# Squares of four chunks added on GpSimd ahead of TensorE's column sums, and the last block's last weights in two token halves

## The reference

```
def rmsnorm(x, g):
    xf = x.astype(jnp.float32)
    y = xf * lax.rsqrt(jnp.mean(xf * xf, axis=-1, keepdims=True) + EPS)
    return (y * g.astype(jnp.float32)).astype(x.dtype)
...
for l in range(DEPTH):
    mod = (jax.nn.silu(cond) @ ada_w[l] + ada_b[l])[:, None, :]
    sh_m, sc_m, g_m, sh_f, sc_f, g_f = jnp.split(mod, N_MOD, axis=-1)
    h = rmsnorm(x, norm_mix_g[l]) * (1.0 + sc_m) + sh_m
    ...
    x = x + g_m * y
    h = rmsnorm(x, norm_ffn_g[l]) * (1.0 + sc_f) + sh_f
    x = x + g_f * (jnp.square(jax.nn.relu(h @ ffn_w1[l])) @ ffn_w2[l])
return rmsnorm(x, final_norm_g), outs_f, outs_b
```

## Time and profile before

| | |
|---|---|
| median of the runs shown (lowest) | 1217.7 us (1216.96) |
| the profiled execution | 1218.6 us |
| its span on the slowest core (core 2) | 1217.3 us; the others 1211.5 to 1215.9 |
| PE / DVE / ACT / POOL busy | 1110.2 / 461.1 / 423.4 / 112.8 us |
| mean granted TensorE clock | 0.981 of 2.4 GHz on core 2, 0.983 to 0.985 on the others |

### The profile page before, as it was taken

The page is one execution under the profiler, slowest core; times in us unless marked ns, Lnnn a source line. Parts: engine busy times, 40 slices in busy tenths (PEclk is TensorE's granted clock), DMA queues, the critical chain, the costliest instruction groups (busy, mean ns, idle before and its releaser), DMA issues.

```text
span 1217.3 us, 16072 instructions; the slowest of 8 cores (1211.5 to 1217.3 us)
## 1 busy us (share of the span) xinstructions
PE 1110.2 (91%) x6516; PEld 552.7 (45%) x6516; DVE 461.1 (38%) x817; ACT 423.4 (35%) x789; POOL 112.8 (9%) x150
## 2 busy tenths in 40 slices
PE   0368998887999999999999999999999999999996
PEld 0133576665444444444444444443444444444442
DVE  0333477676464222222222444825532222222235
ACT  1355576664465320013310551124643100332022
POOL 0122355442000000000000000000000000000000
PEclk9988999998999999999999999999999999999998
DMA  9870844338116844854674344141403431340004
GB/s 163 159 186 1 146 88 123 68 72 212 66 37 103 137 72 69 138 97 69 113 125 70 49 69 69 35 75 30 68 3 69 69 48 22 70 70 1 1 32 176
DMA packets 13446, 99.46 MB, mean 82 GB/s; under 512 B 1499, under 2 KB 5083, under 8 KB 7356
## 3 DMA queue, kind: packets, MB, share of 16 engines
q0 software_dynamic: 6272, 78.91, 37.8%
q1 hardware_dynamic: 7100, 19.52, 4.8%
HBM read 165.27 MB, written 7.86 MB: 142 GB/s over the span
## 4 chain that ended last, share of the span: by engine, by line
PE 87%; DVE 3%; DMA 3%; ACT 3%; POOL 2%; issue 1%; SPq 0%; POOLq 0%; ACTq 0%; DVEq 0%
PE psf L322 87%; DMA sb_X<-xT 3%; POOL sb_B L915 1%; ACT sb_hT L336 1%; DVE sb_ntm L342 1%; ACT sb_A L336 1%; DVE sb_B L342 1%; DVE sb_X L342 1%; POOL sb_X L915 0%; DVE sb_A L339 0%; ACT L336 0%; DVE sb_X L339 0%; ACT sb_B L336 0%; PE psf L910 0%; ACT sb_lnr L336 0%
## 5 line engine op out<-in xcount | busy, mean ns | idle before, releaser
L322 PE MATMUL psf<-sb_hT,sb_slot 128*128 128x512 bf16 (+1 forms) x2472 | 557.3, 384 | 32.6 <-ACT sb_hT L336 22.6
L322 PEld LDWEIGHTS psf<-sb_hT,sb_slot 128*128 128x128 bf16 (+1 forms) x2472 | 241.3, 99 | 326.6 <-issue 14.0
L322 PE MATMUL psf<-sb_A,sb_slot 128*128 128x512 bf16 x1632 | 362.3, 380 | 0.0
L322 PEld LDWEIGHTS psf<-sb_A,sb_slot 128*128 128x128 bf16 x1632 | 159.6, 98 | 192.5 <-issue 1.1
L336 ACT ACTIVATE sb_relu<-psf 128x512 bf16<-128x512 f32 x192 | 113.6, 595 | 356.2 <-PE psf L322 356.2
L342 DVE SCALAR_TENSOR_TENSOR sb_X<-psf,sb_modT,sb_X 128x512 f32<-128x512 f32 x144 | 108.1, 750 | 277.7 <-PE psf L322 277.6
L339 DVE TENSOR_TENSOR sb_A<-sb_relu 128x512 bf16<-128x512 bf16 x192 | 81.7, 425 | 240.3 <-ACT sb_relu L336 239.9
L336 ACT ACTIVATE sb_B<-sb_X 128x512 bf16<-128x512 f32 x96 | 57.2, 624 | 193.2 <-DVE sb_X L342 156.6
L322 PE MATMUL psf<-sb_slot,sb_hT 128*128 128x192 bf16 (+2 forms) x672 | 92.2, 292 | 6.3 <-DVE sb_B L342 6.3
L336 ACT ACTIVATE sb_hT<-sb_ntm,sb_modT 128x512 bf16<-128x512 f32 x96 | 67.9, 721 | 38.5 <-DVE sb_ntm L342 37.7
L342 DVE SCALAR_TENSOR_TENSOR sb_ntm<-sb_X,sb_gscT,sb_rstd 128x512 f32<-128x512 f32 x96 | 70.3, 749 | 25.3 <-ACT sb_rstd L336 21.1
(11 more groups left out here) (115 smaller groups left out, 619.7 us busy)
## 6 DMA issues: line engine op xcount, KB each, us to landing
sb_slot<-w POOLq DMA_DIRECT2D x16, 2048.0 KB, 16.0
sb_slot<-adaw POOLq DMA_DIRECT2D x12, 2048.0 KB, 15.3
sb_X<-xT SPq DMA_DIRECT2D x6, 1024.0 KB, 8.5
yT<-sb_X SPq DMA_DIRECT2D x12, 512.0 KB, 2.7
sb_X<-xT POOLq DMA_DIRECT2D x4, 1024.0 KB, 20.2
sb_X<-xT SPq DMA_DIRECT2D x4, 512.0 KB, 28.9
sb_slot<-evH POOLq DMA_DIRECT2D x1, 2048.0 KB, 14.2
sb_slot<-dft SPq DMA_DIRECT2D x1, 2048.0 KB, 15.0
```

Of the source, the lines that this page charges most:

```text
L322: T.op("pe", lambda: nc.tensor.matmul(out, l, r, start=start, stop=stop), reads=R, writes=W, sig=stop if sig is None else sig)
```

## The change

The squares stay on ACT, one for each chunk. In the four later norms POOL then adds the squares of two neighbouring chunks in f32 and two such pairs into one bf16 tile, so that TensorE has one statistic matmul for four chunks (`stat4`). Its lag is 5 groups in `outproj` and 3 in the MLPs' last half, and `norm_end` is put off as far. The first norm keeps `stat`.

In the last `w2` piece of the second MLP the third block (`m = 1`) is done in two halves of 256 tokens (`final_halves`): four groups of 16 matmuls of 256 columns for the first half, then four for the second. The added squares of its channels 0 to 3 are held back (`hold=True`) and go in by one matmul of 256 columns for each half; channels 4 to 7 have a statistic matmul of 256 columns for each chunk and half, with lag 1. `fin` is the final norm of a half: `Ln`, `Exp`, eight DVE operations of 256 columns, and four transfers, of which the second half gives two to ACT's queue.

```
+        def padd(o, a, b):
+            T.op("pool", lambda: nc.gpsimd.tensor_tensor(out=o[0], in0=a[0], in1=b[0], op=ALU.add),
+                 reads=[a[1], b[1]], writes=[o[1]])
+
+        def stat4(m, c, lag, hold=False):
...
+            s_ = qnext("s", 0)
+            act(s_[0], xT[m][:, c, :], AF.Square, [xT_b[m][c]], [s_[1]])
+            st = qr["m"][m]
+            st.append(s_)
+            if c % 2 == 1:
+                a, b = st.pop(), st.pop()
+                o = qnext("p", 1)
+                padd(o, b, a)
+                st.append(o)
+            if c % 4 == 3:
+                a, b = st.pop(), st.pop()
+                o = qnext("q", 2)
+                padd(o, b, a)
+                if hold:
+                    qr["hold"] = o
+                    return
+                pe_defer(lag, lambda: mm(ps[:], onesb[:], o[0], [o[1], on_b], [pb], start=(c == 3), stop=(c == 7), sig=True))
...
-                stat(m, oc, 2)
+                stat4(m, oc, 5)
                 if oc == 7:
                     pend.append(m)
-                    pe_defer(2, lambda: norm_end(m, nxt))
+                    pe_defer(5, lambda: norm_end(m, nxt))
...
+        def final_halves(m, w, slb, aT, aT_b, l):
...
+            def fin(hs, q, sp_, spb):
+                act(lnr[:, hs], sp_[:, hs], AF.Ln, [spb, on_b], [lnr_b], bias=cst[:, 0:1])
+                act(rstd[:, hs], lnr[:, hs], AF.Exp, [lnr_b], [rstd_b], scale=-0.5)
+                for c in range(8):
+                    stt(xT[m][:, c, hs], xT[m][:, c, hs], pp[:, PP_GFIN + c:PP_GFIN + c + 1], rstd[:, hs], ALU.mult, ALU.mult,
+                        [xT_b[m][c], rstd_b, pp_b], [xT_b[m][c]])
+                    if c % 2 == 1:
+                        T.dma("act" if q and c % 4 == 1 else "sp", y_d[m, :, c - 1:c + 1, hs], xT[m][:, c - 1:c + 1, hs], Buf("yst"),
+                              reads=[xT_b[m][c - 1], xT_b[m][c]])
+
+            for hh in range(2):
...
+                pe_defer(0, lambda sp_=sp_, spb=spb, hs=hs: mm(sp_[:, hs], onesb[:], q4[0][:, hs], [q4[1], on_b], [spb],
+                                                               start=True, stop=False, sig=True))
+                for o in range(4):
...
+                    group(ps[:, 0:256], [(w[:, kc, o * 128:(o + 1) * 128], aT[:, kc, ts_]) for kc in range(16)],
+                          [slb] + [aT_b[kc][m] for kc in range(16)], [pb])
+                    stt(xT[m][:, oc, hs], ps[:, 0:256], modT[l][:, 40 + oc, ci:ci + 1], xT[m][:, oc, hs], ALU.mult, ALU.add,
+                        [pb, mod_b[l][5]], [xT_b[m][oc]])
+                    s_ = qnext("s", 0)
+                    act(s_[0][:, 0:256], xT[m][:, oc, hs], AF.Square, [xT_b[m][oc]], [s_[1]])
+                    pe_defer(1, lambda s_=s_, hs=hs, oc=oc, sp_=sp_, spb=spb: mm(sp_[:, hs], onesb[:], s_[0][:, 0:256], [s_[1], on_b], [spb],
+                                                              start=False, stop=(oc == 7), sig=True))
+                if hh == 0:
+                    pe_defer(1, lambda hs=hs, sp_=sp_, spb=spb: (side_all(), fin(hs, 0, sp_, spb)))
+                else:
+                    pe_flush()
+                    side_all()
+                    fin(hs, 1, sp_, spb)
...
                             if last:
-                                stat(m, oc, 1)
+                                if nxt == "final" and mi == 2:
+                                    stat1(m, oc, 1)
+                                else:
+                                    stat4(m, oc, 3)
                                 if mi < 2:
-                                    stat(MO[mi + 1], o, 0)
+                                    stat4(MO[mi + 1], o, 3, hold=(nxt == "final" and mi == 1))
                             if pre and mi == 2:
-                                stat(MO[0], o, 1)
+                                stat4(MO[0], o, 3)
                         if last:
                             pend.append(m)
-                            pe_defer(1, lambda m=m: norm_end(m, nxt))
+                            pe_defer(1 if nxt == "final" and mi == 2 else 3, lambda m=m: norm_end(m, nxt))
```

More of the change, by code:

```diff
@@ L474, in sq_ring, with quad_ring, qnext, stat1 @@
             return sqr["b"]
+        qr = {}
+        def quad_ring(t, npr, tq, olds):
+            pe_flush()
+            qr["s"] = [(t[:, i * 512:(i + 1) * 512], ab("sq4", olds)) for i in range(4)]
+            qr["p"] = [(t[:, 2048 + i * 1024:2048 + (i + 1) * 1024].bitcast(F32), ab("pr", olds)) for i in range(npr)]
+            qr["q"] = [(tq[:, i * 512:(i + 1) * 512], ab("qd", olds)) for i in range(3)]
+            qr["n"] = [0, 0, 0]
+            qr["m"] = {}
+            return [b for k in "spq" for _, b in qr[k]]
+        def qnext(k, i):
+            n = qr["n"][i]
+            qr["n"][i] += 1
+            return qr[k][n % len(qr[k])]
+        def padd(o, a, b):
+            T.op("pool", lambda: nc.gpsimd.tensor_tensor(out=o[0], in0=a[0], in1=b[0], op=ALU.add),
+                 reads=[a[1], b[1]], writes=[o[1]])
+        def stat4(m, c, lag, hold=False):
+            if c == 0:
+                sbank[m] = (None, None) if hold else PS2()
+                qr["m"][m] = []
+            ps, pb = sbank[m]
+            s_ = qnext("s", 0)
[15 more added lines that the diff above has]
+                pe_defer(lag, lambda: mm(ps[:], onesb[:], o[0], [o[1], on_b], [pb], start=(c == 3), stop=(c == 7), sig=True))
+        def stat1(m, c, lag):
+            ps, pb = sbank[m]
+            s_ = qnext("s", 0)
+            act(s_[0], xT[m][:, c, :], AF.Square, [xT_b[m][c]], [s_[1]])
+            pe_defer(lag, lambda: mm(ps[:], onesb[:], s_[0], [s_[1], on_b], [pb], start=(c == 0), stop=(c == 7), sig=True))
         def stat(m, c, lag, first=None, lastc=None):
@@ L568, in ffn, with side_all @@
+        def side_all():
+            while side:
+                side.pop(0)()
         def ffn(l, nxt):
@@ L608, in ffn @@
                     for mi, m in enumerate(MO):
+                        if last and nxt == "final" and mi == 2:
+                            final_halves(m, w, slb, aT, aT_b, l)
+                            break
                         for o in range(4):
```

20 lines of the change are left out of this document (12 added, 8 removed).

## The result

The changed kernel takes **1230.9 us** (median) against 1218.1 for the kernel before, run beside it: ratio 1.0102, 95% interval 1.0082 to 1.0122. That is 1% slower, where I had forecast 1202.4 us, 1.3% faster; the interval also shows that this kernel's measurement can tell apart less than the 2% that I had named. Ratios leave out executions in which the cores of a die ran at a lower granted clock and took longer, here one of four for each kernel.

The account below looks back on a forecast made before the run. TensorE's matmul work was taken as the bound (87% of the span), DVE and ACT in the tail and `odO`; 14.4 + 3.5 + 0.7 - 3.3 = 15.3 us gave a median of 1202.4 us, range 1196 to 1209.

Parts of the forecast that it names:

- The tail: From block 0's last group to the span's end: 31.0 us in place of 27.7, a loss of 3.3, between 1.6 and 5.3.
- held tile ready at 9: Tail's upper bound: adds longer by 0.5 us, held squares ready at 9 us in place of 6.9, loss 5.3 us.
- 14.4 + 3.5 + 0.7: Gains in us: 14.4 from fewer statistics on TensorE, 3.5 from the wait in `odO`, 0.7 from the wait in `evO`.
- The 0.7 us for the wait in `evO`: Block 0's first group in `evO` would wait less for ACT's copy: gain 0.7 us, between 0 and 1.3.
- the 1.4 us of clock that I had credited: Part of the 3.5 us for `odO`: core 3, 1.4 us behind core 2, would set the time without the wait.
- statistics were filler: Rival: TensorE waits elsewhere for half of the statistics' time, 7.2 us come back, 1209.6 us; chance 0.05.
- the rival in which they are the bound: Rival: each of 69 POOL adds costs its excess over 2.3 us; at 3.1 us an add, 1258 us; chance 0.03.
- POOL and DVE excluding each other: Rival: POOL's adds block DVE fully, `hT` comes late in two places, tail at its upper bound, 1207.8 us; chance 0.15.

Follow-up runs that it names:

- experiment 4: The changed kernel with each norm step's shift on ACT put out one step later than its product on DVE: 1211.4 us, ratio 0.9957.
- experiment 3: The kernel before with only the output projections' lag changed, five groups in place of two, no adds on POOL: 1220.1 us, ratio 1.0028.
- Experiment 7: Two runs, each on top of experiment 4: token halves tracked on their own, 1209.8 us; held adds done one block earlier, 1211.2 us.

## Why the prediction was wrong

**The step that failed** is "The longer lag of `norm_end` moves a block's eight steps three groups back; they end some three groups before the block is needed, so nothing waits." I took the steps at DVE's own pace. They go at 2.36 us a group in the first weights, by the closed chain of ACT and DVE, a period that stood in the trace of before. Thirteen groups at 0.63 over are 8.2 us, against 5.2 of free groups. The runs showed the price: 16.8 us from `evO` on (experiment 4 against the changed kernel), 17.2 between the spans of their profiled executions and 19.4 between the medians. Of these 17.2, 11.3 are waits in the two places; the lower clock behind them is 5 x 0.28 = 1.4 us in the first and, with 0.86 over the next 5 us, 3.6 x 0.50 + 5 x 0.14 = 2.5 us in the second. The lag alone makes 3 us of wait in each place (experiment 3); the rest hangs, as far as the traces tell, on POOL's adds and on TensorE being there sooner. No rival had this chain.

**The tail** was mis-sized: 9.9 us worse in place of 3.3. Its direction and its mechanism (DVE's eight half steps ahead of the second half's sums, TensorE waiting ahead of the last half group) were right: 4.29 us of wait in place of 3.6. What I lacked: the held sum was ready at 9.7 us after block 0's last group, not 6.9, since adds and steps took longer beside each other; the clock fell there already, over 1199 to 1206 it was 0.56; and the transfer (1.5 us). Experiment 7 took these away one at a time: the tail of experiment 4, again 37.6 us, falls to 35.5 with the held sum early and to 34.8 without the transfer's wait. A "held tile ready at 9" was my own upper bound, and without the transfer and this earlier fall of the clock it gave only 5.3. The last half group lost 0.9 us to the clock (2.77 us for 1.91), where I had 1.7. Of the 28.5 us between forecast and median the tail has 6.6, the steps of the norm 16.8 and `evO` (next) 3.0; some 2 have no place.

**The gains were there, but for `evO`.** In experiment 4 block 0's last group ends at 1172.4, where it was 1189.58 before: 17.2 us, where I had 14.4 + 3.5 + 0.7 = 18.6. From the end of the work ahead of `evO` to the first `ada` behind the first weights (small matmuls with `sb_scT` that make `mod`) it is 94.2 us in place of 97.8, and 18 statistics at 0.216 are 3.9. From the start of the last `ada` to the end of block 0's last group it is 517.5 in place of 530.7: 46 statistics, 9.9 us, and 3.5 for `odO` make 13.4 of the 13.2.

So the statistics are worth what I counted, but that the sum nearly comes out is in part luck. The 0.7 us for the wait in `evO` was wrong in sign: the wait changed its releaser and grew by 0.63 us, with 1.7 us of lower clock behind it. Core 2 before, the slowest, had lost as much elsewhere: its first 24 matmuls of `evO` took 8.26 us, those of the other cores 6.40 to 6.82. Against the seven other cores before (909.8 to 910.2 us from `evO` on), experiment 4 (905.5 to 906.2 on all) is 4.3 us shorter with a tail 9.9 longer, so it won 14.2 us ahead of the tail, and not 17.2. Those cores waited the same 2.14 us in `odO` without the 1.4 us of clock that I had credited: 18.6 - 1.4 - 0.7 - 2.3 = 14.2.

The rival "statistics were filler" falls in the version without the waits; in the changed kernel itself all of it was eaten.

**POOL's adds** took 1.15 to 1.39 us on average by form, where I had 1.2 from the earlier trace rows, and POOL is busy 199.1 of 1227.2 us: the rival in which they are the bound (above 2.3 us an add) is out. Two of the four forms:

```profile
L492 POOL TENSOR_TENSOR sb_B<-sb_B 128x512 f32<-128x512 bf16 x34 | 41.3, 1220 | 168.8 <-ACT sb_B L336 163.9 <-DVE sb_hT L339 4.9
L492 POOL TENSOR_TENSOR sb_A<-sb_A 128x512 f32<-128x512 bf16 x12 | 13.8, 1154 | 48.0 <-ACT sb_A L336 48.0
```

**POOL and DVE excluding each other** came nearest to the truth of the rivals: it has "`hT` comes late to the next weights, by some 1.5 us in two places", for a reason that is under half of it at most: 3.1 of the 5.8 us in the first place, and 2.96 of the 5.5 in the second, come without any add.

Not settled: the division of the 5.5 us between the lag, POOL's adds and the earlier arrival of TensorE, of which only the lag's 3 us has a run. Of the last 2 of the 17.2 us, 0.5 stands at the start of `evO` already (304.72 against 304.21), and some 1.2 is seven times 0.17: a group that a wait follows takes 1.90 us, where groups in a row take 1.73.

## What to carry to other kernels

Before a step is moved later, read its period from the trace at the place to which it moves: a step whose parts alternate between two engines, with another stream's work in the same queues, goes at the sum of the four and not at the busy time of either engine. If the period is longer than the group that it hides behind, a later start is paid for; putting out the second half of a step one step later opens the chain at no cost. In a tail, put on the last engine's queue first what lets the next engine go on, and look for transfers that read what the next write is tracked with.
